# Seven products for the output panels of the MLP groups, with the block sums of the hidden activation on GpSimd

## What is computed

```python
h2 = _rmsnorm(x, g_ffn)
x = x + jnp.square(jax.nn.relu(h2 @ w_ff1)) @ w_ff2
gate = jax.nn.sigmoid(_rmsnorm(x, g_ple) @ w_ple_gate)
x = x + gate * (pe @ w_ple_proj)
```

## Time and profile before

| | |
|---|---|
| time, median of 3 runs | 1041.21 us (1040.75 to 1042.89) |
| profiled execution, first to last instruction | 1041.0 us |
| MLP groups on TensorE | 610.5 to 979.5 us |
| busy in the span: PE, DVE, ACT, POOL | 98%, 74%, 50%, 24% |
| a full group (763 to 853 us: panels 5 to 7, then hidden panels and head) | about 90.4 us |

### The profile page before, as it was taken

How to read it: one execution, slowest core, us unless ns; L and a number is a source line. 1 busy time by engine, 2 the same in 40 slices (tenths; PEclk the granted TensorE clock), 3 DMA queues, 4 the chain that set the end, 5 groups by cost and what they waited for, 6 DMA issues and landing times.

```text
span 1041.0 us, 20872 instructions
## 1 busy us (share of the span) xinstructions
PE 1023.5 (98%) x8310; PEld 1008.5 (97%) x8310; DVE 774.4 (74%) x1004; ACT 518.5 (50%) x1253; POOL 245.6 (24%) x381
## 2 busy tenths in 40 slices
PE   9999999999999999999999999999999999999997
PEld 7999999999999999999999989999999999999997
DVE  6679888988899878999674368747856875786553
ACT  6773797658845574352264385414522531453332
POOL 2441233122312003958201211100100100012300
PEclk9999999999999999999999999999999999999999
DMA  6557556776687765776843335655664574573412
GB/s 186 192 178 231 200 177 208 227 242 206 208 256 213 210 218 148 224 218 186 258 142 122 122 122 208 214 183 172 229 209 152 195 247 168 171 252 130 162 54 86
DMA packets 131634, 195.89 MB, mean 188 GB/s; under 512 B 32321, under 2 KB 109473, under 8 KB 129746
## 3 DMA queue, kind: packets, MB, share of 16 engines
q1 hardware_dynamic: 107616, 125.51, 37.9%
q0 software_dynamic: 10560, 63.28, 18.3%
q10 hardware_dynamic: 13362, 5.77, 2.0%
HBM read 185.55 MB, written 62.00 MB: 238 GB/s over the span
## 4 chain that ended last, share of the span: by engine, by line
PE 66%; DVE 13%; ACT 5%; issue 5%; DMA 5%; POOL 3%; SPq 3%; ACTq 0%; DVEq 0%; POOLq 0%
PE gm L1347 26%; PE gm L1603 7%; PE psSO L1603 4%; PE gm L1321 4%; PE gm L1322 3%; PE gm L1323 3%; PE psT L1603 3%; DMA w_raw<-in_w_in 3%; PE psSO L1651 2%; PE psSO L1347 2%; PE psT L1347 2%; PE psT L1651 2%; DVE w_lo L1708 2%; POOL kv L2363 2%; ACT prob L1123 2%
## 5 line engine op out<-in xcount | busy, mean ns | idle before, releaser
L1321 PE MATMUL gm<-w_hi,h_hi 128*128 128x256 f32 x640 | 186.9, 292 | 1.1 <-DVE w_lo L1708 0.9
L1322 PE MATMUL gm<-w_hi,h_lo 128*128 128x256 f32 x640 | 180.8, 282 | 0.0
L1323 PE MATMUL gm<-w_lo,h_hi 128*128 128x256 f32 x640 | 180.1, 281 | 0.0
L1347 PE MATMUL gm<-h_hi,w_hi 128*128 128x272 f32 x624 | 132.7, 294 | 0.4 <-ACT z L852 0.4
L1347 PE MATMUL gm<-h_hi,w_lo 128*128 128x272 f32 x624 | 130.0, 290 | 0.0
L1347 PE MATMUL gm<-h_lo,w_hi 128*128 128x272 f32 x624 | 129.4, 289 | 0.0
L1321 PEld LDWEIGHTS gm<-w_hi,h_hi 128*128 128x128 f32 x640 | 120.8, 189 | 3.1 <-issue 1.7
L1323 PEld LDWEIGHTS gm<-w_lo,h_hi 128*128 128x128 f32 x640 | 121.2, 189 | 0.0
L1322 PEld LDWEIGHTS gm<-w_hi,h_lo 128*128 128x128 f32 x640 | 120.6, 188 | 0.0
L2352 POOL DMA_DIRECT2D out_kvs<-in_cache_kv_w x64 | 35.0, 547 | 345.2 <-PE gm L1347 120.6
L1708 DVE TENSOR_TENSOR w_lo<-w_raw,w_hi 128x1024 fp32r<-128x1024 f32 x76 | 90.5, 1228 | 21.3 <-ACT w_hi L755 20.8
(11 more groups left out here) (378 smaller groups left out, 2662.7 us busy)
## 6 DMA issues: line engine op xcount, KB each, us to landing
out_kvs<-in_cache_kv_w POOLq DMA_DIRECT2D x64, 510.0 KB, 4.7
w_raw<-in_w_in SPq DMA_DIRECT2D x60, 512.0 KB, 6.2
w_raw<-in_w_ff SPq DMA_DIRECT2D x36, 512.0 KB, 5.7
kv<-in_cache_kv_w SPq DMA_DIRECT2D x128, 128.0 KB
kv<-in_cache_kv_w SPq DMA_DIRECT2D x64, 256.0 KB
out_kvs<-in_cache_kv_w POOLq DMA_DIRECT2D x32, 508.0 KB, 5.3
w_more<-in_w_ff SPq DMA_DIRECT2D x26, 512.0 KB, 6.1
kv<-in_cache_kv_w POOLq DMA_DIRECT2D x128, 64.0 KB, 3.3
```

The lines of the kernel that those rows point to most:

```text
L1321: nc.tensor.matmul(out, lh, wh, start=k == 0, stop=False)
L1322: nc.tensor.matmul(out, ll, wh, start=False, stop=False)
L1323: last = nc.tensor.matmul(out, lh, wl, start=False, stop=k == KD - 1)
L1347: last = nc.tensor.matmul(pair[:, half, 0:HALF], w, x[:, k0 + k, half * HALF:(half + 1) * HALF], start=first, stop=end)
```

## The change

- `seven(p)` now holds for panels 5, 6 and 7 of every group too: 12 panels more. The head panel stays ordinary.
- These products need block sums of the hidden activation, anew in each group: `y_hi`, `y_lo`, four of each (t1 to t4). GpSimd makes the sums (`combine_hidden`: two steps of 272 elements for each hidden block, so four a panel; `join_head`: two of 1088 behind the head panel's first half). ScalarE casts them (`combined_hidden_hi`), VectorE subtracts (`combined_hidden_lo`) and makes one difference (`head_difference`). The third sum lies in the columns of `x2` that the head panel has finished with (`head_used`).
- The row factor `rb` is no longer squared and applied at the output, but applied at the hidden blocks with the relu (`relu_parts`, and `hidden_unit`, which now takes the evacuation of ordinary hidden units over from ScalarE). ScalarE then squares twice (`squares`: once into `x2_hi`, once into `z`), instead of casting once. In its queue these squares stand ahead of the second and third copy of a part.
- Output blocks of the head panel are added from PSUM to `xT` in one step (`unit_to_x`); those of panels 5 to 7 by `add_parts` and `parts_to_x`.
- `proj`'s place is used for the sums: it is stored to DRAM at the start of the groups and loaded again after the last product. The last panel's raw weights get a buffer of their own (`w_last`).

The core of the diff:

```diff
 def seven(p):
     j, q = divmod(p - P_FF, FF_PANELS)
-    return P_FF <= p < P_PG and q < 4 and (j > 0 or q >= 2)
+    return P_FF <= p < P_PG and q != 4 and (j > 0 or q >= 2)
...
             def pair_hi(p, hh, n):
-                act.wait_ge(unit_ready, PAIR_FREE[PAIRS[p] + n - 4])
+                if n == 2 and (p - P_FF) % FF_PANELS == 5:
+                    act.wait_ge(head_used, (p - P_FF) // FF_PANELS + 1)
+                else:
+                    act.wait_ge(unit_ready, PAIR_FREE[PAIRS[p] + n - 4])
...
-            def squares_hi(p, m):
+            def squares(p, m):
                 j, uu = divmod(2 * (p - P_FF) + m, FF_UNITS)
-                act.wait_ge(z_used, j * FF_UNITS + zc(U_FF) + uu)
-                nc.scalar.copy(x2_hi[:, uu], z[:, m]).then_inc(hid_hi, 1)
+                act.wait_ge(relu_done, 2 * sum(hidden(x) for x in SEVENS if x < p) + m + 1)
+                nc.scalar.activation(x2_hi[:, uu], z[:, m], ACT.Square).then_inc(hid_hi, 1)
+                act.wait_ge(hid_hi, j * KD + uu + 1)
+                nc.scalar.activation(z[:, m], z[:, m], ACT.Square).then_inc(z_used, 1)
...
+                if before and hidden(p - 1):
+                    squares(p - 1, 0)
+                    squares(p - 1, 1)
+                if q == 3:
+                    combined_hidden_hi(j, 0)
                 if new:
                     part(p, 1)
                     if p == SEVENS[0]:
                         raw_hi(p + 1, 1)
+                    if q == 5:
+                        combined_hidden_hi(j, 2)
                     part(p, 2)
-                if seven(p - 1):
-                    squares_hi(p - 1, 0)
-                    squares_hi(p - 1, 1)
...
+            def combine_hidden(p, m):
+                u = U_FF + 2 * (p - P_FF) + m
+                j, uu = divmod(u - U_FF, FF_UNITS)
+                src = z[:, m] if seven(p) else sqf[:, uu % 2]
+                first, second = src[:, 0:HALF], src[:, HALF:NT]
+                pool.wait_ge(z_used, zc(u))
+                k = uu % 4
+                if uu < 4:
+                    if u == U_FF:
+                        pool.wait_ge(proj_out, 16)
+                    gp.tensor_tensor(y_sum[0][:, k], first, second, ALU.subtract).then_inc(y_summed, 1)
+                    gp.tensor_tensor(y_sum[1][:, k], first, second, ALU.subtract).then_inc(y_second, 1)
+                else:
+                    pool.wait_ge(y_second, 8 * j + uu)
+                    gp.tensor_tensor(y_sum[1][:, k], y_sum[1][:, k], second, ALU.add).then_inc(y_second, 1)
+                    pool.wait_ge(y_second, 8 * j + uu + 1)
+                    gp.tensor_tensor(y_third_sum[k][:], y_sum[1][:, k], first, ALU.subtract).then_inc(y_third, 1)
+
+            def join_head(j):
+                pool.wait_ge(head_used, j + 1)
+                pool.wait_ge(hid_lo, KD * (j + 1))
+                link(gp.tensor_tensor(y_sum[2], x2_lo[:, 4:8, HALF:NT].bitcast(F32), y_lo[2].bitcast(F32), ALU.subtract))
+                pool.wait_ge(y_joined, 2 * j + 1)
+                gp.tensor_tensor(y_sum[2], y_sum[2], y_sum[3], ALU.add).then_inc(y_joined, 1)
```

More of the change, by code:

```diff
@@ L93, in zc @@
 def zc(u):
-    return sum(STAGED[:u + 1]) + max(0, u + 1 - U_FF)
+    return sum(STAGED[:u + 1]) + sum(x >= U_PG or (x - U_FF) % FF_UNITS < KD for x in range(U_FF, u + 1))
 def panel_end(p):
@@ L1200, in hidden_panel @@
                 j, q = divmod(p - P_FF, FF_PANELS)
-                new, after = seven(p), seven(p + 1)
-                if seven(p - 1):
+                new, after, before = seven(p), seven(p + 1), seven(p - 1)
+                if before:
                     part(p - 1, 3)
-                if new and not seven(p - 1):
+                if p == SEVENS[0]:
                     sums_hi(p, 0, 2)
@@ L2209, in hidden_panel @@
                 j, q = divmod(p - P_FF, FF_PANELS)
-                new, after = seven(p), seven(p + 1)
-                if seven(p - 1) and not new:
+                new, after, before = seven(p), seven(p + 1), seven(p - 1)
+                if before and not new:
                     add_parts(p - 1, 0)
-                if new and not seven(p - 1):
+                if p == SEVENS[0]:
                     pair_lo(p, 0, 2)
```

264 lines of the change are left out of this document (193 added, 71 removed).

## The result

The changed kernel takes **1102.38 us** (median of 4 runs, 1101.94 to 1107.61), beside 1042.05 us (1040.75 to 1044.13) for the kernel before on the same chip: 1.058 times as long, 95% interval 1.054 to 1.062. The forecast was 1080 us with a range of 1046 to 1092. The direction was right, the size was not, by 22 us. The profiled execution has a span of 1100.1 us; it is 59.1 us longer than that of before, where the forecast had 39.0.

A forecast was written before the change was run, and what follows sets the result against it. The MLP was taken to go at TensorE's pace, with VectorE next; -17.4 (matmuls) + 28.8 (head stretch) + 17.1 (hidden panels) + 8.5 (group 0) + 2 (start and end) = +39.0, so 1080 us, range 1046 to 1092.

The forecast's parts named there:

- head stretch: VectorE's work from TensorE's start of panel 4 to y_lo2: 28.4 us against 21.1, 7.2 us wait a group, +28.8.
- group 0: First group: VectorE now evacuates its ordinary hidden units, 6.1 us, and GpSimd's additions cost 2.4: +8.5 (bounds 6.1 and 10).
- 28.8 + 17.1 + 8.5 + 2: Added us, in order: head stretch of four groups, hidden panels of groups 1 to 3, group 0, start and end.
- removed matmuls: Panels 5, 6, 7 of four groups fall from 96 to 84 matmuls: -17.4 us if all else keeps up.
- two bounds of the head stretch: Over four groups: 7.2 us of waiting if GpSimd costs nothing, 28.8 with its additions; the upper was taken.
- The lock: VectorE and GpSimd, both reading SBUF, wait for each other's whole instruction: VectorE loses 0.48 us per short addition, 2.4 per long.
- lockstep: A waiting GpSimd instruction goes in between two steps of a full VectorE queue.
- the clock: Rival: TensorE's clock falls behind waits of 2.5 to 4 us, twice a group: 4 to 12 us more, 1084 to 1092; chance 0.14.
- +2: Start and end: GpSimd additions and VectorE's steps delay the sum of squares after the last group: +2 us (0 to 4).
- No lock: Rival: GpSimd's short additions do not hold VectorE up: +6.5, so 1048; a share between gives 1050 to 1068; together 0.24.
- p3 waits: Hidden panels, groups 1 to 3: sixth product waits for ScalarE's copy, 3.2 us a group without GpSimd, 5.7 with: +17.1.
- Faster: Rival: VectorE keeps its lead, all removed products pay, waits are a few in group 0 only: 1030 us; chance 0.08.

The follow-up runs named there:

- e1: The changed kernel with every block sum of GpSimd left out, zeros written by memset instead (values not the reference's): 1063.8 us.
- e3: The changed kernel with idle matmuls (fillers) added ahead of two long TensorE waits, in hidden panel 2 (groups 1 to 3) and panel 5 (all groups): 1093.6 us.
- e13: The changed kernel with another order of ScalarE's and VectorE's steps in the last panel of the last group alone: 1105.6 us.
- e4: The changed kernel with VectorE's subtraction that makes y_lo2 moved to the front in output panel 5: 1101.6 us.
- e9: The changed kernel with VectorE's addition of the first block's parts moved ahead of the 1024-element subtraction in six panels of a group: 1102.4 us.

## Why the prediction was right and where it failed

**The waits were right.** In group 1 TensorE waits 0.16 + 2.61 + 1.79 for copies and 1.23 + 1.91 + 3.92 in the head stretch: 4.6 and 7.1 us. The forecast had 5.7 and 7.2. In group 0 the waits grew by 14.9 us against 7.2 + 8.5 = 15.7. Over all stages they grew by 54.0 us; the forecast's terms for them are 28.8 + 17.1 + 8.5 + 2 = 56.4. (By its own terms the wait of the head stretch is 28.4 - 21.1 = 7.3 and not 7.2, 0.4 us over four groups.) The removed matmuls, the two bounds of the head stretch (1.82 in e1 for the lower one) and the choice of the upper one held.

**The lock was right, its share a little low.** The forecast's upper less its lower terms make 28.8 - 7.2 + 17.1 - 9.6 + 2.4 + 1 = 32.5 us; leaving the sums out gave 38.6, in which some low clock is gone too. It stated lockstep, one GpSimd instruction between two of VectorE; that happens in one lap and not in the next (below).

**The step that failed is the clock.** The sum put what TensorE loses behind its waits at nothing. The clock stood as a rival with 0.14, worth 4 to 12 us, beside a sum without it. But the forecast itself had waits of 2.5 to 4 us, and the earlier trace rows showed the fall behind one of 1.52: by its own rows the clock belonged in the sum. How much: against the forecast the stages are longer by 6.4 (group 0: 17.8 measured, 11.4 forecast), 3.4 and 3.4 (groups 1 and 2: 12.0 and 8.6) and 6.9 us (group 3 with the last stage: 17.5 and 10.6), 20.1 together (the other 2 us of the 22 are the spread of the executions: the two profiled ones differ by 59.1 us, the median of this one and the one forecast from by 61.2). What is not wait in these stages (their growth, and the 4.35 us of removed matmuls, less the growth of the waits) is 7.2, 4.7, 4.7 and 5.9 us, 22.5 together, so the whole miss lies outside the waits. How it divides is an estimate. From the granted clock of the stages (0.89 of 62.4, 0.97 of 53.1, 102.4, 102.4 and 106.8 us) at most some 18 us of it are half clock (length times what the clock lacks of 1.00; part of it lies inside waits), more than the rival's 12; the rest would be some 0.2 us that each of 25 waits costs beyond its listed length (the product at 793.23 takes 3.64 us to the next start, of which 1.91 is wait and 1.51 a product's time). What an experiment shows of it are the 8.8 us that fillers at seven places gave back (e3).

**The last group was undersized.** +2 was forecast for the end; the waits there are 4.3 us longer than in the groups before. y_lo2 is 5.36 us late there instead of 3.92, as GpSimd also adds the rows' Squares in the head stretch, and the first gate unit waits 2.87 us for its banks, a wait that was not in the forecast; group 3 takes 4.4 us more than group 2 and the last stage 1.0 more than before. e13 showed that the second wait covers another, for the sum of squares, which is the one the forecast had named.

**Group 0** was right as a sum of waits, 14.9 against 15.7, and 6 us short: the longest wait stands there, with the longest stretch of half clock behind it.

**The rivals.** "No lock" (1048) was tested by e1 itself and came to 1063.8: the lower bounds of the head stretch and of the p3 waits held there too. The granted clock of group 1 was 0.98 there, group 0 still waited 3.81 and 1.50 us for w_lo, and the first gate unit 3.83 us; how the 16 us divide among these was not worked out. "Faster" (1030) stays far even without GpSimd, with a better order and ScalarE's relu (1052.2).

## What to carry to other kernels

Removing work from the bounding engine pays only as far as the next engine can follow place by place; here 4.35 us of matmuls a group were bought with 26 us more busy time a group on VectorE, 9 of them only waiting for GpSimd. If a forecast contains many waits of the matmul engine that are as long as one behind which the trace shows the clock at half, the clock belongs in the sum and not among the rivals, even if it does not fall behind every one of them. And a wait that is removed by order alone should be followed to where the lateness goes next: three of these edits gained nothing (e4, e9, e13), and two of them together gained 11 us.
